# Twelve RMS norms of a two-block model: sums of squares in token columns, the root on 128x4 values, and the factor spread over the rows by a TensorE product

## The chip, the cores and the metric

The kernel runs on one core of a Trainium2 chip. The metric is the device time of one execution in microseconds, lower is better. A core has five engines that run side by side and meet at semaphores: TensorE (matrix products, PE in the profile, its weight loads PEld), VectorE (DVE), ScalarE (ACT), GpSimd (POOL) and SyncE (SP, which issues most transfers). SBUF is the working memory with 128 rows; TensorE writes only to PSUM, here eight banks of 128x512 fp32.

## The reference, cut to what matters

512 tokens of width 1024 go through two blocks, everything in fp32. Block one has two layers (latent attention, then attention with forget gates), each with a memory attention and an output projection whose result is normed and added to `x`. Block two has two layers, each a mixer and a gated feed-forward part, with a modulated norm ahead of each, and a norm at the end. Every norm is this one:

```python
def rms_norm(x, g):
    xf = x.astype(jnp.float32)
    y = xf * lax.rsqrt(jnp.mean(xf * xf, axis=-1, keepdims=True) + EPS)
    return (y * g.astype(jnp.float32)).astype(x.dtype)

def modulate(x, g, shift, scale):
    return (rmsnorm(x, g) * (1.0 + scale) + shift).astype(x.dtype)
```

The norms that the change touches, in order: the 256 memory tokens; `x` ahead of layer one; the query latent (width 384) and the key latent (256); the output of layer one, then `x` ahead of layer two; the output of layer two, then `x` ahead of the even mixer; `x` ahead of the first feed-forward part, of the odd mixer, of the second feed-forward part; the end. Twelve in all.

## The kernel before

The activations lie transposed: features on the 128 rows, tokens along the 512 columns, `x` as eight tiles of 128x512. Projections are fp32 products split in three (high times high, high times low, low times high). Weights arrive in a ring of three chunks; for each chunk ScalarE writes the high half `wh` (L1164), GpSimd the low half `wl` (L2024, 128x2048 for most), and TensorE multiplies (`three`, L505; `out_second`, L950). Two chunks of halves are in hand (SPLIT). Activations are split the same way: ScalarE writes the high half, VectorE the low half (`low`, L1596 or L1598). Each engine's program is written out in order by hand. TensorE takes its PSUM banks in rotation, six of them; bank seven, `ssq_bank`, is kept for the sums of squares and some attention outputs.

A norm goes like this. ScalarE squares a tile (`square`, L1189) into one of two buffers `sq`. TensorE multiplies it by a 128x128 matrix of ones (`ssq`, L532; for the memory L602 and L603), which sums over the features and at once puts the sum on all 128 rows: `ssq_bank` is 128x512. Where a norm is `summed`, VectorE has first added the squares of tiles 0 to 5 (`add_squares`), and TensorE has three products instead of eight (`ssq_summed`, L543). Then VectorE scales by 1/width and adds EPS (L1575), takes the reciprocal (L1578), ScalarE takes the root (`root`, L1202), all 128x512, in the tile `var`, which is also `rstd`. VectorE then multiplies tile by tile: `normed` (L1586), `normed_split` (L1619, with the high half on ScalarE and the low half on VectorE behind each tile), and in `out_first` L1736 for the output of a layer, followed by the addition to `x` (L1739), whose squares feed the next norm.

While this chain runs, TensorE has no projection to do. `warm(count)` (L448) gives it products of the identity with constants, each 512 columns, in fp32, which the profile shows as two passes: seven behind the last sum of an output norm, of the norm behind it and of the norms behind `out_second`, five between the sums of the two latent norms.

The lines around: in `out_first` ScalarE's order is square, copy, weight split (`split_weights`), root; VectorE's order there is the sums of pairs, L1575, L1578, L1736 and L1739 in turn. At the start TensorE does the sums of the memory, then those of `x`, then the memory projections (chunk `mem0`, which wait for nothing from the norm of `x`). In the latent part it does the three sums of the query latent, `warm(5)`, the two sums of the key latent, the rotation of the rotary key (L645), and the gate projections.

## Time and profile before

| | us |
|---|---|
| three runs | 2172.75, 2181.15, 2181.36 (median 2181.15) |
| the profiled execution | 2180.79 |
| its span | 2179.0 |
| TensorE busy | 2062.0 (95%) |
| TensorE loading weights | 1572.6 (72%) |
| VectorE busy | 1053.4 (48%) |
| ScalarE busy | 780.9 (36%) |
| GpSimd busy | 782.9 (36%) |

A line such as L505 is that of a helper, and many places of the program share it. The busy share of TensorE holds the filler products (94.2 us in 212 passes). The granted clock of TensorE is 0.976 in the mean. What a norm costs is not seen in these totals; it is read from the timeline, between the last sum and the first normed tile.

### The profile page before, as it was taken

Reading aid. Unit: us, or ns where it says so; the run is one execution under the profiler, and the core shown is the slowest. Engines: PE = TensorE matmul, PEld = TensorE weight load, DVE = VectorE, ACT = ScalarE, POOL = GpSimd, SP = SyncE. Lnnn points to the kernel's source line nnn. Section 1 sums busy time; section 2 is a strip of 40 time slices with the busy share of each in tenths; the row PEclk is TensorE's granted clock in tenths of the full one; section 3 lists DMA queues with packets and bytes.
Section 4 is the critical chain, followed back from the end, with each engine's and each line's share of the span. In section 5 each row is a group of like instructions: output and inputs, shape, how many; then the busy total and the mean of one; then the engine's idle time right before and its main releaser. Section 6 shows DMA issues by size and latency. Waiting matters only on the chain.

```text
span 2179.0 us, 22946 instructions
## 1 busy us (share of the span) xinstructions
PE 2062.0 (95%) x9468; PEld 1572.6 (72%) x9468; DVE 1053.4 (48%) x1507; ACT 780.9 (36%) x1186; POOL 782.9 (36%) x333
## 2 busy tenths in 40 slices
PE   7998999889999999997999998999999999999998
PEld 5765667588856679884778877886975577788886
DVE  6356575654466666914275546635601343211233
ACT  3332564423355332135342312324355433322231
POOL 3313363134354344221234334433423233434432
PEclk9999999999989999998999999999999999999999
DMA  5226202155510244110125344423311022233321
GB/s 177 90 89 161 78 1 68 60 175 173 174 59 21 97 135 136 59 59 20 58 77 160 111 134 137 149 90 97 97 59 39 20 97 78 78 97 98 108 62 62
DMA packets 202728, 203.54 MB, mean 93 GB/s; under 512 B 11871, under 2 KB 199523, under 8 KB 202624
## 3 DMA queue, kind: packets, MB, share of 16 engines
q1 hardware_dynamic: 200953, 200.90, 28.9%
q0 software_dynamic: 656, 1.01, 0.3%
q8 instruction: 75, 1.23, 0.3%
q10 hardware_dynamic: 1015, 0.16, 0.0%
q14 instruction: 29, 0.24, 0.0%
HBM read 199.10 MB, written 2.10 MB: 92 GB/s over the span
## 4 chain that ended last, share of the span: by engine, by line
PE 69%; DVE 14%; ACT 7%; POOL 6%; DMA 2%; issue 2%; SPq 0%; DVEq 0%; ACTq 0%; POOLq 0%
PE bank L505 40%; PE bank L950 14%; POOL wl L2024 6%; ACT wh L1164 3%; PE bank L687 2%; DVE var L1578 2%; DVE acc L1546 2%; PE bank L711 1%; PE bank L807 1%; PE bank L736 1%; DVE conv L1917 1%; DVE conv L1919 1%; PE bank L1009 1%; DVE conv L1915 1%; PE bank L1030 1%
## 5 line engine op out<-in xcount | busy, mean ns | idle before, releaser
L2024 POOL TENSOR_TENSOR wl<-ring,wh 128x2048 fp32r<-128x2048 f32 (+3 forms) x150 | 643.0, 4288 | 1099.3 <-ACT wh L1164 1099.3
L1164 ACT ACTIVATE wh<-ring 128x2048 fp32r<-128x2048 f32 (+3 forms) x150 | 265.1, 1768 | 286.1 <-PE bank L950 95.3
L1546 DVE SCALAR_TENSOR_TENSOR acc<-ring,cs,acc 128x256 f32<-128x256 f32 x336 | 287.5, 856 | 12.0
L505 PE MATMUL bank<-xfh,wh 128*128 128x512 f32 x704 | 278.2, 395 | 15.6 <-POOL wl L2024 12.7
L505 PE MATMUL bank<-xfh,wl 128*128 128x512 f32 x704 | 275.0, 391 | 0.0
L505 PE MATMUL bank<-xfl,wh 128*128 128x512 f32 x704 | 274.9, 391 | 0.0
L505 PEld LDWEIGHTS bank<-xfh,wh 128*128 128x128 f32 x704 | 132.6, 188 | 51.1 <-POOL wl L2024 17.4
L505 PEld LDWEIGHTS bank<-xfh,wl 128*128 128x128 f32 x704 | 132.6, 188 | 28.2
L1894 DVE SCALAR_TENSOR_TENSOR x<-bank,mod,x 128x512 f32<-128x512 f32 x48 | 34.7, 750 | 243.0 <-PE bank L950 243.0
L505 PEld LDWEIGHTS bank<-xfl,wh 128*128 128x128 f32 x704 | 132.8, 189 | 26.6
L950 PE MATMUL bank<-hsph,wh 128*128 128x512 f32 x352 | 138.8, 394 | 4.7 <-POOL wl L2024 4.7
L950 PE MATMUL bank<-hsph,wl 128*128 128x512 f32 x352 | 138.0, 392 | 0.0
L950 PE MATMUL bank<-hspl,wh 128*128 128x512 f32 x352 | 137.9, 392 | 0.0
L2043 POOL TENSOR_SCALAR probs<-probs,rinv 128x256 f32<-128x256 f32 (+2 forms) x96 | 95.4, 1007 | 70.1 <-DVE rinv L1713 70.1
L1915 DVE TENSOR_SCALAR conv<-a_raw,vecs 128x512 f32<-128x512 f32 x44 | 23.9, 544 | 192.4 <-ACT a_raw L1170 192.4
L1170 ACT ACTIVATE a_raw<-bank 128x512 f32<-128x512 f32 x44 | 26.5, 602 | 194.0 <-PE bank L505 192.2
L448 PE MATMUL bank<-consts 128*128 128x512 f32 x212 | 94.2, 593 | 0.0
L1544 DVE TENSOR_SCALAR acc<-ring,cs 128x256 f32<-128x256 f32 x48 | 24.3, 507 | 141.7 <-PE bank L495 131.7
L1280 ACT ACTIVATE probs<-bank,nmx 128x256 f32<-128x256 f32 (+3 forms) x128 | 64.5, 512 | 59.4 <-DVE nmx L1710 59.3
L1189 ACT ACTIVATE sq<-x 128x512 f32<-128x512 f32 x56 | 35.1, 630 | 129.2 <-DVE x L1894 116.1
L950 PEld LDWEIGHTS bank<-hsph,wh 128*128 128x128 f32 x352 | 66.8, 190 | 19.0 <-issue 4.8
L505 PE MATMUL bank<-xbh,wh 128*128 128x512 f32 x184 | 73.6, 400 | 3.6 <-DVE xbl L1596 3.6
(386 smaller groups left out, 4277.4 us busy)
## 6 DMA issues: line engine op xcount, KB each, us to landing
ring<-in_ada_w SPq DMA_DIRECT2D x48, 1024.0 KB, 5.3
ring<-in_ffn_w_in SPq DMA_DIRECT2D x44, 1024.0 KB, 5.2
ring<-in_w_in_b SPq DMA_DIRECT2D x14, 1024.0 KB, 5.3
ring<-in_even_w_in SPq DMA_DIRECT2D x14, 1024.0 KB, 5.2
ring<-in_ffn_w_out SPq DMA_DIRECT2D x16, 768.0 KB, 4.9
ring<-in_odd_w_in SPq DMA_DIRECT2D x12, 1024.0 KB, 5.3
ring<-in_ffn_w_out SPq DMA_DIRECT2D x16, 640.0 KB, 4.4
ring<-in_w_out SPq DMA_DIRECT2D x8, 1024.0 KB, 5.1
```

Source lines behind the costliest of these rows:

```text
L448: eng.matmul(b[:, :], ident, consts[:, 0:S], start=True, stop=True)
L505: mm = eng.matmul(o, l_, r_, start=(first and i == 0), stop=(last and i == 2))
L687: eng.matmul(b[:, at_col:at_col + n], qf[0:kd, h, i * P:n], kf[0:kd, h, 0:n], start=first, stop=False, skip_group_check=True)
L950: mm = eng.matmul(b[:, :], ws[a_][:, k, t * P:(t + 1) * P], xs[b_][:, k0 + k, :], start=(first and j == 0), stop=(end and j == 2))
L1164: eng.activation(wh[:, m % SPLIT, 0:w], ring[:, n % RING, 0:w], ACT.Copy).then_inc(wh_ready, 1)
L1189: eng.activation(sq[:, i % 2, :], src, ACT.Square).then_inc(sq_ready, 1)
L1280: ins = eng.activation(probs[:, par, po:po + n], b[:, c:c + n], ACT.Exp, bias=nmx[:, par, i:i + 1], scale=scale, accum_out=rsum[:, par, i: ...
L1546: ins = eng.scalar_tensor_tensor(out=s, in0=w[:, k, :], scalar=cs[:, k:k + 1], in1=s, op0=ALU.mult, op1=ALU.add)
L1578: eng.reciprocal(var[:, 0:n], var[:, 0:n]).then_inc(var_ready, 1)
L1915: chain.link(eng.tensor_scalar(u, r[:, 0:S], vec(name, t), vec("ffn_conv_b_2", FT * l + t), ALU.mult, ALU.add))
L2024: eng.tensor_tensor(wl[:, m % SPLIT, 0:w], ring[:, n % RING, 0:w], wh[:, m % SPLIT, 0:w].bitcast(F32), ALU.subtract).then_inc(wl_ready, 1)
L2043: eng.tensor_scalar(w, w, rinv[:, par, i:i + 1], None, ALU.mult).then_inc(probs_ready, 1)
```

## The change

- `token_sums` takes the place of the product with 128x128 ones. The square is now the stationary operand, 128 tokens at a time, and one column of ones the moving one: four products of one column for each tile. `ssq_bank` then holds 128x4 values (128x2 for the memory): the sum of token 128j+p on row p, column j.
- Scaling, reciprocal and root work on `rcol`, 128x4.
- VectorE writes `var`, 128x512: the identity times the column j of `rcol`, four diagonals side by side (`diag_ready`).
- TensorE multiplies ones by these diagonals (`spread`) into a rotating bank: the factor of each token on all rows. A `spread` stands in TensorE's program behind the sums of each norm: for the memory ahead of the sums of `x`, for `x` ahead of the memory projections, and for the two latent norms both behind the second latent's sums.
- `normed_split` and `out_first` read the factor from that bank, `normed` copies it to `var` first. The last tile frees the bank, so it counts on `emptied["dve"]` in place of `scaled` or `post_scaled`; waits and counts on the other engines follow.
- The filler: 7 and 7 in `out_first` become 1, spread, 2, and 1, spread, 2 (`OUT_FILL`), with one product of 256 columns behind each of the first seven sums of `x`; 7 behind `out_second` become 1, spread, 2.

```diff
@@ TensorE
-            def warm(count, aside=False):
+            def warm(count, aside=False, n=S):
@@
-                    eng.matmul(b[:, :], ident, consts[:, 0:S], start=True, stop=True)
+                    eng.matmul(b[:, 0:n], ident, consts[:, 0:n], start=True, stop=True)
@@
+            def token_sums(src, first, last, fold=1):
+                blocks = NB // fold
+                for j in range(NB):
+                    mm = eng.matmul(ssq_bank[:, j % blocks:j % blocks + 1], src[:, j * P:(j + 1) * P], ones[:, 0:1],
+                                    start=(first and j == 0), stop=(last and j >= NB - blocks),
+                                    skip_group_check=True)
+                mm.then_inc(sq_used, 1)
@@ ssq
-                eng.matmul(ssq_bank[:, :], ones, sq[:, i % 2, :], start=(t == 0), stop=(t == total - 1)
-                           ).then_inc(sq_used, 1)
+                token_sums(sq[:, i % 2, :], t == 0, t == total - 1)
                 counts["sq"] += 1
+            def spread(n=S):
+                k = counts["spread"]
+                b = bank(("rs", k), "dve")
+                pe.wait_ge(diag_ready, k + 1)
+                done(eng.matmul(b[:, 0:n], ones, var[:, 0:n], start=True, stop=True))
+                counts["spread"] += 1
@@ the start
             counts["hn"] += 1
+            spread(M)
             for k in range(KT):
                 ssq(k, KT)
+            spread()
@@ the latent norms
             warm(5)
             for t in range(2):
                 ssq(t, 2)
+            spread()
+            spread()
@@ out_first
                 ssq_summed()
-                warm(7)
+                warm(OUT_FILL[0])
+                spread()
+                warm(OUT_FILL[1])
                 for t in range(KT):
                     ssq(t, KT)
-                warm(7)
+                    if t < KT - 1:
+                        warm(1, n=M)
+                warm(OUT_FILL[2])
+                spread()
+                warm(OUT_FILL[3])
@@ out_second
                 if last:
                     ssq_summed()
-                    warm(7)
+                    warm(1)
+                    spread()
+                    warm(2)
@@ ScalarE, root
-                eng.activation(rstd[:, 0:n], var[:, 0:n], ACT.Sqrt).then_inc(rstd_ready, 1)
+                eng.activation(rcol[:, 0:n // P], rcol[:, 0:n // P], ACT.Sqrt).then_inc(rstd_ready, 1)
@@ VectorE, inverse
-                eng.tensor_scalar(var[:, 0:n], ssq_bank[:, 0:n], 1.0 / width, EPS, ALU.mult, ALU.add
+                cols = slice(0, n // P)
+                eng.tensor_scalar(rcol[:, cols], ssq_bank[:, cols], 1.0 / width, EPS, ALU.mult, ALU.add
                                   ).then_inc(ssq_taken, 1)
                 dve.wait_ge(ssq_taken, k + 1)
-                eng.reciprocal(var[:, 0:n], var[:, 0:n]).then_inc(var_ready, 1)
+                eng.reciprocal(rcol[:, cols], rcol[:, cols]).then_inc(var_ready, 1)
                 used["norm"] += 1
+                dve.wait_ge(rstd_ready, k + 1)
+                shape = [P, n // P, P]
+                eng.tensor_tensor(var[:, 0:n].rearrange("p (b q) -> p b q", q=P), ident.unsqueeze(1).to_broadcast(shape),
+                                  rcol[:, cols].unsqueeze(2).to_broadcast(shape), ALU.mult).then_inc(diag_ready, 1)
+                return take(dve, ("rs", k), "dve")
@@ normed
-                inverse(count, width, n, squares)
-                dve.wait_ge(rstd_ready, used["norm"])
+                b = inverse(count, width, n, squares)
+                eng.tensor_copy(var[:, 0:n], b[:, 0:n]).then_inc(emptied["dve"], 1)
+                wait_emptied(dve, ("rs", used["norm"] - 1))
@@ normed_split
-                    eng.scalar_tensor_tensor(out=tmp[:, t % 2, :], in0=x[:, t, :], scalar=g, in1=rstd[:, :],
-                                             op0=ALU.mult, op1=ALU.mult).then_inc(scaled, 1)
+                    eng.scalar_tensor_tensor(out=tmp[:, t % 2, :], in0=x[:, t, :], scalar=g, in1=rs[:, :],
+                                             op0=ALU.mult, op1=ALU.mult
+                                             ).then_inc(scaled if t < KT - 1 else emptied["dve"], 1)
@@ out_first
-                        eng.tensor_tensor(o1[:, t, :], o1[:, t, :], rstd[:, :], ALU.mult).then_inc(post_scaled, 1)
+                        eng.tensor_tensor(o1[:, t, :], o1[:, t, :], rs[:, :], ALU.mult
+                                          ).then_inc(post_scaled if t < KT - 1 else emptied["dve"], 1)
```

## Rows read from the trace of the kernel before

**Rows 1.** The chain that ended last, by engine, from the page.
```profile
PE 69%; DVE 14%; ACT 7%; POOL 6%; DMA 2%; issue 2%; SPq 0%; DVEq 0%; ACTq 0%; POOLq 0%
```

**Rows 2.** Groups by line and shape; busy us, mean ns, idle before.
```profile
L1578 DVE RECIPROCAL var<-var 128x512 f32<-128x512 f32 x11 | 36.9, 3353 | 0.4
```

**Rows 3.** Timeline, norm ahead of the first feed-forward part; start us, length us, what.
```profile
1089.44 0.30 PEld L532 LDWEIGHTS bank<-sq,consts 128*128 128x128 f32 x2 [0.61 <-ACT sq L1189]
...
1090.60 0.69 DVE L1575 TENSOR_SCALAR var<-bank 128x512 f32<-128x512 f32 x1 [1.88 <-PE bank L532]
...
1091.20 1.28 ACT L1202 ACT_TABLE_LOAD   x1
...
1091.26 4.51 POOL L2024 TENSOR_TENSOR wl<-ring,wh 128x2048 fp32r<-128x2048 f32 x1 [6.28 <-ACT wh L1164]
1091.33 3.35 DVE L1578 RECIPROCAL var<-var 128x512 f32<-128x512 f32 x1
...
1095.38 1.61 DVE L1619 SCALAR_TENSOR_TENSOR tmp_f<-x,gmod,var 128x512 f32<-128x512 f32 x2 [0.70 <-ACT var L1202]
```

**Rows 4.** Timeline, operations of 128x4 values at 776 us.
```profile
775.85 0.20 ACT L1360 ACTIVATE lbt<-lbt 128x4 f32<-128x4 f32 x1
...
776.09 0.18 DVE L1787 RECIPROCAL lbt<-lbt 128x4 f32<-128x4 f32 x1 [0.69 <-ACT lbt L1360]
```

**Rows 5.** Timeline at 49 and at 1145 us: GpSimd and VectorE at once.
```profile
48.97 4.51 POOL L2024 TENSOR_TENSOR wl<-ring,wh 128x2048 fp32r<-128x2048 f32 x1 [14.92 <-ACT wh L1164]
...
49.45 4.59 DVE L1596 TENSOR_TENSOR xal<-tmp_a,xah 128x512 fp32r<-128x512 f32 x1 [0.65 <-ACT xah L1176]
...
1145.29 5.03 POOL L2024 TENSOR_TENSOR wl<-ring,wh 128x2048 fp32r<-128x2048 f32 x1 [1.44 <-ACT wh L1164]
...
1145.99 1.29 DVE L1937 TENSOR_TENSOR prod<-bank,gel 128x512 f32<-128x512 f32 x2
```

**Rows 6.** Timeline of the output norm of layer one and the norm behind it.
```profile
390.34 4.51 POOL L2024 TENSOR_TENSOR wl<-ring,wh 128x2048 fp32r<-128x2048 f32 x1 [9.33 <-ACT wh L1164]
...
395.08 1.29 DVE L1736 TENSOR_TENSOR o<-o,var 128x512 f32<-128x512 f32 x2 [0.70 <-ACT var L1202]
...
397.69 0.30 PEld L532 LDWEIGHTS bank<-sq,consts 128*128 128x128 f32 x2 [2.25 <-ACT sq L1189]
...
398.90 0.30 PEld L532 LDWEIGHTS bank<-sq,consts 128*128 128x128 f32 x2 [0.91 <-ACT sq L1189]
...
406.94 0.69 DVE L1575 TENSOR_SCALAR var<-bank 128x512 f32<-128x512 f32 x1 [2.13 <-PE bank L532]
```

**Rows 7.** Timeline, four products with one moving column, eight weight loads.
```profile
194.06 1.09 PEld L495 LDWEIGHTS bank<-consts,acc 128*128 128x128 f32 x8
```

**Rows 8.** Timeline, a product with 256 moving columns, its two weight loads.
```profile
21.22 0.41 PEld L602 LDWEIGHTS bank<-sq,consts 128*128 128x128 f32 x2
```

**Rows 9.** Timeline of the two latent norms: last filler pass, first tiles.
```profile
131.05 0.19 PEld L448 LDWEIGHTS bank<-consts 128*128 128x128 f32 x1 [0.24 <-issue]
...
132.59 2.08 DVE L1586 SCALAR_TENSOR_TENSOR cq<-cq,vecs,var 128x512 f32<-128x512 f32 x3 [0.70 <-ACT var L1202]
...
141.16 1.41 DVE L1586 SCALAR_TENSOR_TENSOR ckv<-ckv,vecs,var 128x512 f32<-128x512 f32 x2 [0.70 <-ACT var L1202]
```

**Rows 10.** Timeline, the first memory projection.
```profile
37.55 0.19 PEld L505 LDWEIGHTS bank<-memh,wh 128*128 128x128 f32 x1 [2.46 <-issue]
```

**Rows 11.** Stretches: length; busy PE, PEld, DVE, ACT, POOL; PEclk, DMA share, GB/s.
```profile
788.50:792.70 4.20, 0.23 (x3) 0.14 (x2) 3.54 (x1) 1.15 (x3) 4.20 (x1) 0.75 0.75 238
790.60:797.40 6.80, 4.64 (x11) 3.67 (x12) 6.66 (x5) 3.19 (x2) 5.44 (x2) 0.50 0.59 193
397.70:406.00 8.30, 7.83 (x15) 2.38 (x16) 7.11 (x12) 4.41 (x7) 0.00 (x0) 1.00 0.20 69
```

**Rows 12.** Groups by line and shape: a factor from a bank, and from SBUF.
```profile
L1894 DVE SCALAR_TENSOR_TENSOR x<-bank,mod,x 128x512 f32<-128x512 f32 x48 | 34.7, 750 | 243.0 <-PE bank L950 243.0
...
L1619 DVE SCALAR_TENSOR_TENSOR tmp_f<-x,gmod,var 128x512 f32<-128x512 f32 x16 | 12.2, 775 | 1.8 <-ACT var L1202 1.4
```

49 lines of the change are left out of this document (27 added, 22 removed).

## The prediction

> **What bounds the kernel now.** I read the page first. The chain that ended last is TensorE work for 69% [rows 1], so at most places a change on VectorE or ScalarE costs nothing. The norms are the exception: between the last square and the first normed tile no projection can run. TensorE looks busy there, but only with `warm` filler. So I read each of the twelve norms in the timeline and asked what is late there. The largest item is the reciprocal, 3.353 us for 128x512, 11 times [rows 2]. In the norm ahead of the first feed-forward layer [rows 3] the last sum starts at 1089.44, the scaling (L1575) at 1090.60, the reciprocal at 1091.33, and the first normed tile at 1095.38: 4.78 us from the start of the scaling to the first tile. Two more things stand in these rows. ScalarE loads the table of the root at 1091.20 for 1.28 us, ready at 1092.48, which the reciprocal hides. GpSimd makes the low half of a weight chunk from 1091.26 to 1095.77.
>
> **Part 1, the chain without waits.** Scaling, reciprocal and root shrink to 128x4. The nearest rows are a 128x4 reciprocal, 0.18, and a 128x4 activation, 0.20 [rows 4]; for the scaling, which reads PSUM, I take 0.20 (bounds 0.16 to 0.69, the row before). Added are a 128x512 product onto the diagonals, 0.69 like every fp32 product here, and a TensorE product over 512 columns plus its wait. The old last sum had the same shape and took 1.16 from its first load to VectorE's start (1089.44 to 1090.60 [rows 3]). With 0.04 for each hand-over: 0.20+0.18+0.20+0.69+1.16+0.17 = 2.6 us instead of 4.78, 2.2 saved. `normed` copies the result out of PSUM first, 0.73 more, which leaves 1.4.
>
> **Part 2, the waiting product, the step that decides.** The diagonal product reads two tensors from SBUF, `ident` and `rcol`. Such an operation stands still here while GpSimd makes a low half: GpSimd works 48.97 to 53.48, and a 0.69 us subtraction issued at 49.45 takes 4.59, ending 0.55 after GpSimd. The product L1937, with one operand in PSUM, is not touched at 1145.99 in the middle of a GpSimd subtraction [rows 5]. The old chain was of the second kind (PSUM input, then a reciprocal, which ran at 3.35 under GpSimd [rows 3]). The new one can't start its product before the root, 1092.48+0.20, and GpSimd took hold at 1091.26. So it ends at 1095.77+0.55 = 1096.32, `ones` is loaded at 1096.37, and the first tile starts at 1097.53, not 1095.38. The old first tile was itself held a little (two tiles took 1.61), the new one isn't: the net is +1.95. The same picture holds before the odd mixer and the second feed-forward layer: three times. The Trainium skill, "SBUF — State Buffer", section "SBUF: two separate sides", says that a VectorE operation with two SBUF inputs and a GpSimd operation that reads SBUF exclude each other for the whole instruction. By that rule the broadcast operands, which no row here has in such a product, make no difference.
>
> After the output projections of block one GpSimd sits the same way, 390.34 to 394.85, and the first product of the old chain is at 395.08 [rows 6]. New: 394.85+0.55+0.05+1.16 = 396.61, +1.5. Behind it eight squares go to TensorE. They came every 1.21 us (397.69, 398.90), the last one 7.93 after the first, and the next scaling stood at 406.94. A sum is now four one-column products, eight loads. The loads of such products [rows 7] take 1.09 for eight with the last one's 0.19, so 0.90 to 1.0 a sum; its result is later by 0.13. The old sum took 0.86, so the sums by themselves cost nothing. But behind each stands a 256-column `warm`, two passes 0.22 apart [rows 8], 0.43. TensorE's period becomes 1.33, over VectorE's 1.21: 7 x 1.33 = 9.3 instead of 7.9. The second scaling is at 397.69+1.5+9.3+1.3 = 409.8, +2.9. That second norm has no GpSimd work near it and its table is loaded, so it earns 2.2. Net +0.7, twice.
>
> **Part 3, the order on TensorE.** In the latent norms `spread` stands behind the filler and the second sum. The filler's last pass begins at 131.05 [rows 9] and ends at 131.48; two sums, 133.3; product and hand-over, 134.5; copy, 135.2. The first tile was at 132.59: +2.6. The second of them then earns 1.4, and its first tile, 141.16, comes 1.2 late; a weight split waits behind it on ScalarE. At the start of the kernel the memory projection ran from 37.55 [rows 10] beside the norm of x. It now stands behind that norm's `spread`. I put the last squares 3 us later (the sums of x wait for the memory's `spread`, itself behind GpSimd), the projection at 43.2, and the next low half, which waits for ScalarE to empty it, 2.9 us later. Bounds for the start are 0 (the order hidden in the filler) and 6 (the whole shift passed on); I take 2.9 because ScalarE's queue, not TensorE's, fed the next chunk. The final norm earns 2.2-0.13-0.73 = 1.3.
>
> **Part 4, filler and clock.** `warm(7)` becomes one or two products around the spread. After the last sum and one filler TensorE has no work from about 1091.2 until 1096.4, and from 390.8 until 395.4. Gaps of that size cost clock in this trace: 4.2 us without work from 788.5, a mean grant of 0.75 inside, and then 6.8 us at 0.50 [rows 11], the lower level, 1.2 GHz. I counted seven gaps of 4.3 us or more behind the start of the kernel, and all seven show it. The sums of the output norm, about 70% dense from 397.7, hold 1.00. The new gaps are 4.6 (two), about 5.6 (three) and 6 (the latent norms). At the lower level the spread's two passes take 0.9 longer, right on the path: +0.9 for the latent norms, and three times +0.95 for the norms ahead of wide projections, which VectorE paces afterwards, so only 0 to 0.5 more there. After the output projections `warm(2)` takes 3.4 instead of 1.7 and holds up the first sums: +1.9 each.
>
> Reading the spread factor from PSUM I cost at nothing: 750 ns for the 128x512 scalar-tensor-tensor from a bank, 775 in the mean from SBUF [rows 12]. The Trainium skill, "VectorE: DVE Perf Modes", in the section on the TRN2 errata, gives a fixed part of 120 cycles for a PSUM source and 58 for SBUF; by that 64 tiles would cost some 4 us more (an estimate). The rows don't show it.
>
> **The sum.** Start 2.9, latent norms 1.2+0.9 = 2.1, output norms 2 x (0.7+1.9) = 5.2, three modulated norms 3 x (1.95+0.95) = 8.7, end -1.3: +17.6 us. I see no wait for a transfer that would absorb it: DMA is 2% of the chain, and the transfers follow VectorE's steps, which shift too. The profiled execution took 2180.79 (span 2179.0), 0.36 below the median of three. 2181.15+17.6 = 2198.8.
>
> **Rivals.**
> A. As above: 2199, 50%.
> B. The product is held, but the clock stays at 1.00. For it: the fillers were thinned, not dropped. Against: seven gaps of seven. 2.9+1.2+1.4+5.9-1.3 = +10.1: 2191, 20%.
> C, not slower: VectorE gets its access before GpSimd, or a broadcast operand doesn't count. The product would run as soon as the root is there, 1092.72; first tile 1094.6, -0.95 with the old hold, three times. After the output projections -1.4 before the sums, 0 after them, -2.2 behind the second norm, twice. 2.9+1.2-4.4-2.9-1.3 = -4.5: 2177, 15%. It decides if the product starts within a microsecond of the root. Against it: every two-SBUF product issued inside a low half in this trace was held.
> D, the change does what its chain promises everywhere: 12 x 2.2 less four copies of 0.73 = -23: 2158, 7%. It needs C and also that the order at the start and in the latent norms is hidden.
> E. More loss: the clock stays low through the sums and the first projection chunk, the start gives 6, or PSUM reads cost more: about +30, 2211, 8%.
>
> **Range and chances.** A and B hold 70%; to leave out no more than 2 in 10, C must be in: 2174 to 2212. A's own range is 2193 to 2206. A measurement tells about 0.5%, 11 us. Faster by more: D and a little of C, 10%. Within: most of C, half of B, the low edge of A, 30%. Slower: 60%.
>
> **What would show it.** The diagonal product 4 us long, or ending 0.5 us behind GpSimd, in five norms, and 0.69 in the others; first tiles near 1097.5 in place of 1095.4; sums 0.9 long, 1.33 apart in the output norms; granted clock 0.50 for 3 to 7 us behind each. If the product is 0.69 everywhere, the prediction is wrong at part 2; if the clock stays 1.00, at part 4.

## The result, and the profile after

| | before | after |
|---|---|---|
| median of the runs, us | 2179.18 (4 runs) | 2226.66 (4 runs) |
| range | 2172.75 to 2181.36 | 2223.54 to 2227.21 |
| ratio | | 1.022, 95% interval 1.0195 to 1.0245 |
| span of the profiled execution | 2179.0 | 2224.4 |
| TensorE's mean granted clock | 0.976 | 0.949 |

Slower, as forecast, but by 47 us and not by 17.6. 2226.66 lies outside the range of 2174 to 2212. First the page: its busy times, and the rows of the 40 slices for TensorE and its clock.

```profile
PE 2090.6 (94%) x9754; PEld 1623.9 (73%) x9754; DVE 1028.6 (46%) x1523; ACT 775.5 (35%) x1186; POOL 783.6 (35%) x333
...
PE   6989999989999999996999998998999999999998
...
PEclk7989999799999989998999999999999889999999
```

VectorE lost 25 us of work (1053.4 to 1028.6), which is what the change was made of. TensorE gained 29 (2062.0 to 2090.6) and stayed the engine that bounds. The mean clock gives the size of the matter: each us at the lower level (1.2 GHz, granted 0.50) takes half a us from the mean, so 2179.0 us at 0.976 hold 105 us of it, and 2224.4 us at 0.949 hold 227 us. The time at the lower level has doubled.

Next the timeline of the norm ahead of the first feed-forward layer in after, the one that [rows 3] show of before; here and below the columns are start, length, engine, line, operation, output and input, with the idle time before it and what ended that in brackets.

```profile
1120.88 0.16 DVE L1611 TENSOR_SCALAR rcol<-bank 128x4 f32<-128x4 f32 x1 [1.82 <-PE bank L531]
1121.08 0.18 DVE L1614 RECIPROCAL rcol<-rcol 128x4 f32<-128x4 f32 x1
1121.55 1.28 ACT L1234 ACT_TABLE_LOAD   x1
1121.61 4.50 POOL L2066 TENSOR_TENSOR wl<-ring,wh 128x2048 fp32r<-128x2048 f32 x1 [6.26 <-ACT wh L1192]
1122.84 0.20 ACT L1234 ACTIVATE rcol<-rcol 128x4 f32<-128x4 f32 x1
1123.08 3.57 DVE L1618 TENSOR_TENSOR var<-consts,rcol 128x512 f32<-128x512 f32 x1 [1.82 <-ACT rcol L1234]
1126.13 0.37 SPq L1162 DMA_DIRECT2D ring<-in_ffn_w_in  x1
1126.70 2.07 PE L551 MATMUL bank<-var,consts 128*128 128x512 f32 x2 [4.53 <-DVE var L1618]
1128.57 3.37 PE L450 MATMUL bank<-consts 128*128 128x512 f32 x4
1128.82 1.41 DVE L1657 SCALAR_TENSOR_TENSOR tmp_f<-x,gmod,bank 128x512 f32<-128x512 f32 x2 [2.17 <-PE bank L551]
```

This is the held product. It starts at 1123.08, inside GpSimd's low half (1121.61 to 1126.11), and ends at 1126.65, 0.54 behind it. Its work is 0.69, it took 3.57. From scaling to first tile there are 7.94 us, in [rows 3] 4.78: +3.2, of which 0.9 is the spread at the lower clock.

Now the token sums, which the prediction had called free. The first view is of TensorE's weight loads, at the start of the kernel and in the norm behind the output of layer one:

```profile
30.36 13.98 PEld L531 LDWEIGHTS bank<-consts,sq 128*128 128x128 f32 x64
...
422.29 1.08 PEld L531 LDWEIGHTS bank<-consts,sq 128*128 128x128 f32 x8
423.28 0.30 PEld L450 LDWEIGHTS bank<-consts 128*128 128x128 f32 x2
...
427.42 2.04 PEld L531 LDWEIGHTS bank<-consts,sq 128*128 128x128 f32 x8
429.34 0.55 PEld L450 LDWEIGHTS bank<-consts 128*128 128x128 f32 x2
429.98 2.04 PEld L531 LDWEIGHTS bank<-consts,sq 128*128 128x128 f32 x8
...
437.26 0.16 DVE L1611 TENSOR_SCALAR rcol<-bank 128x4 f32<-128x4 f32 x1 [9.96 <-PE bank L531]
```

The second view is of the same stretches and, in its last row, of the same sums in the norm behind the output of layer two: window and length; busy PE, PEld, DVE, ACT, POOL; granted clock, DMA share, GB/s.

```profile
29.70:44.00 14.30, 14.20 (x65) 14.05 (x65) 7.94 (x15) 6.03 (x14) 4.34 (x1) 0.50 0.48 148
421.60:425.00 3.40, 3.40 (x27) 3.27 (x27) 3.40 (x7) 1.39 (x3) 0.00 (x0) 1.00 0.01 2
425.00:437.30 12.30, 12.30 (x51) 11.49 (x50) 2.34 (x5) 2.39 (x4) 0.00 (x0) 0.50 0.00 0
776.60:786.80 10.20, 10.06 (x72) 8.91 (x71) 8.63 (x17) 5.04 (x8) 0.00 (x0) 1.00 0.01 2
```

At full clock a sum and its 256-column filler have a period of 1.32 (422.29 to 423.61), as forecast. At 425.0 the clock falls to 0.50 with TensorE busy 100% of the time, and the period becomes 2.56 (427.42 to 429.98), twice VectorE's 1.2 per tile. It had been at 0.50 from 411.3 to 421.6 too, behind the wait for the held product, and was back at 1.00 for the 3.4 us of the second row. One layer on the same sums keep 1.00 for 10.2 us, and the clock falls at 786.8, ahead of the last of the eight. At the start 64 loads take 13.98 us, one each 0.218, with TensorE busy 14.20 of 14.30 and the clock at 0.50 throughout; there it was low already when the sums began (from 25.6, in a gap of TensorE), and didn't come back while they ran. The engine looks full and runs at half its clock. That is the term that was missing.

To see where the time comes from I subtracted, for each of the 7200 passes of the split projections, its start in before from its start in the other kernel. The lateness (us) at some landmarks, given by their time in before. The columns x_a, x_b, x_even, ffn0 and ffn1 are the first passes on the normed `x` of layer one, layer two, the even mixer and the two feed-forward parts; 183.3 is a later chunk on x_a; x_odd lies 25 us behind the first pass on that of the odd mixer; 342.4 and 694.0 are the first passes of the two output projections. Kernels below the first row are those of the experiments:

| at | x_a 79.5 | first gate chunk 138.3 | 183.3 | 342.4 | x_b 414.0 | 694.0 | x_even 765.9 | ffn0 1098.0 | x_odd 1520.6 | ffn1 1791.3 |
|---|---|---|---|---|---|---|---|---|---|---|
| after | 8.3 | 22.6 | 17.2 | 20.1 | 29.2 | 24.6 | 29.6 | 33.2 | 36.4 | 46.0 |
| early_old | 0.0 | 0.0 | 0.1 | 1.0 | 6.0 | -4.0 | 2.7 | 6.3 | 10.0 | 19.4 |
| early_new | 7.8 | 22.1 | 16.5 | 19.5 | 22.1 | 19.3 | 22.1 | 19.5 | 19.5 | 19.5 |
| sums_128 | 6.4 | 17.5 | 11.3 | 14.7 | 17.6 | 6.8 | 9.2 | 10.0 | 12.9 | 22.5 |
| act_diag | 9.8 | 24.6 | 18.9 | 22.4 | 31.2 | 26.0 | 34.7 | 35.8 | 35.9 | 38.3 |
| root_first | 8.7 | 23.0 | 17.5 | 18.2 | 29.7 | 27.4 | 37.7 | 38.0 | 37.8 | 38.1 |
| order_1 | 8.1 | 8.9 | 20.7 | 23.2 | 28.2 | 25.5 | 34.6 | 35.9 | 37.8 | 45.4 |
| order_128 | 2.1 | -0.4 | 11.2 | 8.3 | 9.7 | 8.0 | 9.5 | 11.3 | 11.5 | 17.7 |
| combo | 0.7 | 0.7 | 0.6 | 0.8 | -0.5 | -10.0 | -11.3 | -13.0 | -14.3 | -11.1 |
| combo_table | 2.2 | 2.2 | 2.2 | 2.4 | 0.4 | -8.4 | -10.4 | -12.6 | -14.5 | -9.7 |
| combo_root | -0.3 | 1.3 | 1.9 | 2.1 | 5.1 | -5.0 | -3.6 | -1.0 | 0.8 | 5.9 |

Each row is one execution, so not every step is the edit's. The one of act_diag is the slowest of its four and 5 us above their median, that of combo is of the faster of its two groups of runs. The attention of layer two (414 to 694) is the same code in all of them. In before's profile the clock is at 0.50 from 609.7 to 626.8 with TensorE busy 17.10 of 17.10. In combo's it is 1.00 there:

```profile
600.00:650.00 50.00, 47.93 (x264) 28.27 (x264) 36.88 (x107) 32.24 (x113) 30.06 (x30) 1.00 0.20 64
```

That alone is about 9 us, and early_old, sums_128 and the three combos have it at that place. In the table sums_128 gains 6.2 us on after between 414.0 and 694.0 in this way, where their code is the same. So steps are read at the norms, where the rows of the timeline explain them, and sizes are taken from medians.

### The profile page after: what moved, and what is told of

Read it like the earlier page. It is cut to its first block, busy times and chain, and to the rows that moved or that the text cites. A ratio compares the mean times of both kernels' runs of the same rounds, so it can differ in the third digit from the quotient of the medians.

```text
span 2224.4 us, 23539 instructions
## 1 busy us (share of the span) xinstructions
PE 2090.6 (94%) x9754; PEld 1623.9 (73%) x9754; DVE 1028.6 (46%) x1523; ACT 775.5 (35%) x1186; POOL 783.6 (35%) x333
## 3 DMA queue, kind: packets, MB, share of 16 engines
q1 hardware_dynamic: 200953, 200.90, 28.2%
q8 instruction: 77, 1.26, 0.2%
## 4 chain that ended last, share of the span: by engine, by line
PE 72%; DVE 11%; ACT 7%; POOL 6%; DMA 2%; issue 2%; SPq 0%; DVEq 0%; ACTq 0%; POOLq 0%
PE bank L507 40%; PE bank L976 13%; POOL wl L2066 5%; ACT wh L1192 3%; PE bank L707 2%; PE bank L450 2%; PE bank L531 2%; DVE acc L1581 2%; PE bank L731 1%; DVE conv L1959 1%; PE bank L833 1%; DVE conv L1961 1%; PE bank L756 1%; PE bank L551 1%; DVE var L1618 1%
## 5 line engine op out<-in xcount | busy, mean ns | idle before, releaser
L1581 DVE SCALAR_TENSOR_TENSOR acc<-ring,cs,acc 128x256 f32<-128x256 f32 x336 | 282.8, 842 | 12.0
L1936 DVE SCALAR_TENSOR_TENSOR x<-bank,mod,x 128x512 f32<-128x512 f32 x48 | 34.7, 751 | 244.2 <-PE bank L976 244.2
L450 PE MATMUL bank<-consts 128*128 128x512 f32 (+1 forms) x176 | 96.7, 683 | 0.0
L976 PEld LDWEIGHTS bank<-hsph,wh 128*128 128x128 f32 x352 | 66.8, 190 | 19.3 <-issue 4.8
L976 PEld LDWEIGHTS bank<-hsph,wl 128*128 128x128 f32 x352 | 66.7, 190 | 14.0
```

Source lines behind the costliest of these rows:

```text
L450: eng.matmul(b[:, 0:n], ident, consts[:, 0:n], start=True, stop=True)
L976: mm = eng.matmul(b[:, :], ws[a_][:, k, t * P:(t + 1) * P], xs[b_][:, k0 + k, :], start=(first and j == 0), stop=(end and j == 2))
L1581: ins = eng.scalar_tensor_tensor(out=s, in0=w[:, k, :], scalar=cs[:, k:k + 1], in1=s, op0=ALU.mult, op1=ALU.add)
L1936: eng.scalar_tensor_tensor(out=x[:, t, :], in0=b[:, :], scalar=mod[:, col:col + 1], in1=x[:, t, :], op0=ALU.mult, op1=ALU.add).then_inc(em ...
```

## The experiments

The theory now had two parts. The held product costs, as predicted. And sums of one moving column let the clock fall although TensorE is never idle. The rivals: it is the thinned filler that lets the clock fall; or it is the order of TensorE's program at the start.

**early_old**: the first four norms as in before, the other eight as in after. The edit gives every norm both forms and picks by its number:

```diff
+NEW = (4, 5, 6, 7, 8, 9, 10, 11)
-                token_sums(sq[:, i % 2, :], t == 0, t == total - 1)
+                if counts["hn"] - 1 in NEW:
+                    token_sums(sq[:, i % 2, :], t == 0, t == total - 1)
+                else:
+                    eng.matmul(ssq_bank[:, :], ones, sq[:, i % 2, :], start=(t == 0), stop=(t == total - 1)
+                               ).then_inc(sq_used, 1)
...
```

> The changed kernel with its first four norms (memory, x, the two latents) made as before, the other eight as changed. The trace of the changed kernel shows the projections 19.6 us late at 206 us, ahead of the first attention. If that shift is made by the first four norms and nothing later takes it back, this run is about 19 us faster than the changed kernel: near 2208. If my prediction's sizes for these norms were right (2.9+2.1 = 5 us) and the rest is chance of the clock, it is near 2222.

Measured: 2196.6 (2192.2 to 2199.4), ratio 1.0073 [1.005, 1.0096], 30 us below after, and 11 below the 2208 expected. Taking the first four norms back to the old form gives back more than half of the loss. In the table after is 17 to 20 us late between 183.3 and 342.4, where I had counted 5.0. What it has beyond these comes next, in stretches that are the same in both kernels: 4.1 at the first output norm (steps of 9.1 and 5.0), 5.4 in the attention of layer two.

**early_new**: the other half, `NEW = (0, 1, 2, 3)`.

> Only the first four norms (memory, x, the two latents) as in the changed kernel, the other eight as before. Theory (parts add as the two traces show them side by side, 19.6 us of lateness where the second layer begins, some of it absorbed in the attention behind): 2195 to 2201, and the sum with early_old's 15 leaves about 10 of the changed kernel's 47 us to a loss that needs both. Rival (the losses of the two halves add to the whole): 2209 to 2214.

Measured: 2202.8 (2201.5 to 2208.7), ratio 1.0124 [1.0093, 1.0154]: +24.0 over the median of before in that comparison. With early_old's +15.4 that makes 39.4 of the 47.5. It fits neither number exactly: between the theory's 2201 and the rival's 2209, nearer to the theory. The 8 us that only both together lose have one visible part. In early_old seven of the eight sums of the norm behind layer one's output ran at full clock, 1.33 apart, and the clock fell at 411.6:

```profile
402.60 0.97 PEld L539 LDWEIGHTS bank<-consts,sq 128*128 128x128 f32 x8 [0.98 <-ACT sq L1244]
...
410.44 1.08 PEld L539 LDWEIGHTS bank<-consts,sq 128*128 128x128 f32 x8
```

so that the output norm and the next cost 5.0 us there (1.0 to 6.0 in the table), in after 9.1 (20.1 to 29.2). The same instructions lost the clock 9 us into the sums here and 5 us into them in after. What decides that I can't say from these runs.

**sums_128**: the ones are the moving operand with 128 columns and not with one. The sums are the same, 128 times over, and the scaling reads each 128th column. Nothing else is changed.

```diff
-                    mm = eng.matmul(ssq_bank[:, j % blocks:j % blocks + 1], src[:, j * P:(j + 1) * P], ones[:, 0:1],
+                    mm = eng.matmul(ssq_bank[:, (j % blocks) * P:(j % blocks) * P + 128], src[:, j * P:(j + 1) * P], ones[:, 0:128],
...
-                eng.tensor_scalar(rcol[:, cols], ssq_bank[:, cols], 1.0 / width, EPS, ALU.mult, ALU.add
+                eng.tensor_scalar(rcol[:, cols], ssq_bank[:, 0:n:P], 1.0 / width, EPS, ALU.mult, ALU.add
```

> The changed kernel with one edit: each product of the sums has 128 columns of ones moving instead of one, so the weight loads are the same, 0.112 us apart at full clock, and 128 columns are worked on behind each. Theory A (the clock falls because the one-column sums work on hardly any columns, though the profile calls the engine busy): the sums of x at the start, 64 loads in 13.98 us at a grant of 0.50, take about 7.3; the sums of x behind the output norm of layer one stay at 1.00; 10 to 15 us faster than the changed kernel, 2212 to 2217. Theory B (only the gaps without work lower the clock): the same stretches at 0.50 as in the changed kernel, and 2223 to 2229.

Measured: 2202.2 (2200.8 to 2205.4), ratio 1.0102 [1.0083, 1.0122]. Giving TensorE 128 times the columns made the kernel 24.4 us faster, more than the theory's 10 to 15. The 64 loads at the start now take 10.21 us, not the 7.3 expected; the clock is low for the first part only (mean grant 0.79 from 28 to 44, in after 0.50 from 29.7 to 44), and the sums of the output norm run at full clock to the end:

```profile
30.87 10.21 PEld L531 LDWEIGHTS bank<-consts,sq 128*128 128x128 f32 x64
...
28.00:44.00 16.00, 10.96 (x66) 10.47 (x66) 9.80 (x21) 8.06 (x18) 6.54 (x2) 0.79 0.42 132
...
425.49 1.08 PEld L531 LDWEIGHTS bank<-consts,sq 128*128 128x128 f32 x8
426.80 0.16 DVE L1611 TENSOR_SCALAR rcol<-bank 128x4 f32<-128x4 f32 x1 [3.38 <-PE bank L531]
```

A sum of eight loads takes 1.08 us at full clock with one column (after, 422.29 above) and with 128: the loads set the pace, and the columns are free. So the difference of 24.4 us can only be the clock and what hangs on it. How much of it lies in the sums is less sure: by the table 5.4 us come before 342.4, 6.2 at the first output norm, 6.2 in the untouched attention of layer two and 5.7 behind it. Without the attention it is some 18 us, an estimate from two single executions.

The traces of all kernels settle the direction. At the two output norms, each with 64 one-column products and fillers between them, six kernels (after, early_old, act_diag, root_first, order_1, fillers) give twelve stretches of sums. The clock fell inside eleven of them, and in the twelfth, of root_first, 0.4 ahead of its first load; it was low for 2.3 to 19.7 us of each. The six kernels with 128 columns (sums_128, order_128, the four combos) give twelve as well, and it fell inside none; in three it was low already when the sums began, for 1.4 to 6.2 us of them, and came back. At the start of the kernel the clock stays at 0.50 through all 14.0 us of one-column sums in five kernels, and with 128 columns it is back after 4.5 to 5.4 us in three.

**fillers**: one-column sums, but with six fillers in front of the spreads of the memory, the two output norms and the norms behind `out_second`, and five in front of the key latent's. The other four spreads stay as in after.

```diff
-OUT_FILL = (1, 2, 1, 2)
+OUT_FILL = (6, 2, 1, 2)
...
+            warm(6)
             spread(M)
...
+            warm(5)
             spread()
...
-                    warm(1)
+                    warm(6)
                     spread()
```

> The changed kernel with more filler: six products in place of one ahead of the spreads that wait for the held product (output norms, and the norms behind out_second), six ahead of the memory's spread, five between the two latent spreads. The order and the sums are as changed. Theory A (one-column sums lower the clock by themselves): the gaps hold 1.00, the spreads there take 1.2 instead of 2.2 us, but the sums of x at the start and behind the output norm still fall to 0.50; 5 to 10 us faster than the changed kernel, 2217 to 2222. Theory B (the gaps alone): the sums stay at 1.00 too, about 20 us faster, 2207.

Measured: 2217.3 (2212.9 to 2227.7), ratio 1.0176 [1.0144, 1.0208]. The clock theory's 2217 to 2222, not the rival's 2207. The six fillers at the start close the gap ahead of the sums, and these rows are the plainest of all: the clock is at 1.00 when the 64 loads begin at 30.84, and falls at 34.4 with TensorE busy without a break. The third row is of the norm behind layer two's output, at 0.50 with TensorE busy all the time:

```profile
29.00:34.40 5.40, 5.40 (x38) 4.40 (x36) 3.52 (x5) 1.72 (x3) 4.79 (x2) 1.00 0.59 194
34.40:48.00 13.60, 11.78 (x50) 10.69 (x51) 8.47 (x22) 5.98 (x15) 0.00 (x0) 0.50 0.26 78
...
764.90:785.40 20.50, 20.50 (x67) 15.67 (x66) 7.79 (x17) 4.69 (x8) 0.00 (x0) 0.50 0.00 0
```

Filler that replaces idle time gave back 9.4 us, columns in the sums 24.4. One of the four runs, at 2227.7, is no faster than after, so the size of the 9.4 is rough; that the thinned filler is the smaller part holds.

**act_diag**: ScalarE writes the diagonals, four copies of the identity scaled by a column, so that VectorE has no product of two SBUF tensors there.

```diff
                 eng.activation(rcol[:, 0:n // P], rcol[:, 0:n // P], ACT.Sqrt).then_inc(rstd_ready, 1)
+                act.wait_ge(rstd_ready, k + 1)
+                for j in range(n // P):
+                    ins = eng.activation(var[:, j * P:(j + 1) * P], ident, ACT.Copy, scale=rcol[:, j:j + 1])
+                ins.then_inc(diag_ready, 1)
...
-                eng.tensor_tensor(var[:, 0:n].rearrange("p (b q) -> p b q", q=P), ident.unsqueeze(1).to_broadcast(shape),
-                                  rcol[:, cols].unsqueeze(2).to_broadcast(shape), ALU.mult).then_inc(diag_ready, 1)
```

> The changed kernel with one edit: the diagonals are written by ScalarE right behind the root, four copies of the identity's 128 columns, each scaled by a column of rcol, so nothing of the chain can be held by GpSimd. If the hold costs what the trace shows (products of 3.57 to 4.99 us in five norms): spread's loads start 2.3 to 3.7 us sooner in these five, the gap without TensorE work falls from 5.2 to 5.9 us to about 3, some of them keep the clock, and the other seven norms pay 0.6 us each for the four copies: near 2212. If the hold is covered by something else that is late: 2226 to 2230.

Measured: 2213.8 (2207.6 to 2218.7), ratio 1.0144 [1.0118, 1.017], 12.9 below after. The timeline of the norm ahead of the first feed-forward layer:

```profile
1126.49 4.50 POOL L2066 TENSOR_TENSOR wl<-ring,wh 128x2048 fp32r<-128x2048 f32 x1 [6.26 <-ACT wh L1192]
...
1127.96 1.28 ACT L1237 ACTIVATE var<-consts,rcol 128x128 f32<-128x128 f32 x4
...
1131.41 1.41 DVE L1657 SCALAR_TENSOR_TENSOR tmp_f<-x,gmod,bank 128x512 f32<-128x512 f32 x2 [5.26 <-PE bank L551]
```

ScalarE wrote all four in 1.28 us in the middle of a GpSimd low half and wasn't held. In the table the three steps of after at ffn0, x_odd and ffn1 (3.6, 3.2, 9.6) are 1.1, 0.1 and 2.4. At the output norms nothing came back: their steps are 8.8 and 8.7 against 9.1 and 5.0, though scaling to first tile is 2.3 shorter in both. In the second of them the clock falls at 781.4 and not at 786.8.

**root_first**: the same hold taken off the product by time. ScalarE takes the root ahead of the weight chunk's high half, so GpSimd's low half comes after the product.

```diff
-                split_weights(tile_chunk[index[(stage, KT - 1)]] + 3)
                 root()
+                split_weights(tile_chunk[index[(stage, KT - 1)]] + 3)
...
-                split_weights(tile_chunk[index[stage + (KT - 1,)]] + 3)
                 root()
+                split_weights(tile_chunk[index[stage + (KT - 1,)]] + 3)
```

> As the changed kernel (2226.7), but ScalarE takes the root ahead of the weight chunk's high half in the two output norms and behind the three second projections, so that GpSimd's low half starts after the diagonal product. Theory (the product is held by GpSimd's low half and by nothing else): the product takes 0.69 in these five norms; first tiles 2.9 earlier three times, 1.5 twice: 2213 to 2217. Rival (the low half comes 2 us later and now holds VectorE's subtractions behind the first tiles, so that it is only moved): the product takes 0.69, but the time stays at 2221 to 2228.

Measured: 2215.7 (2204.9 to 2219.6), ratio 1.0161 [1.0133, 1.0189], 11.0 below after.

```profile
1128.92 0.69 DVE L1618 TENSOR_TENSOR var<-consts,rcol 128x512 f32<-128x512 f32 x1 [0.27 <-ACT rcol L1234]
...
1130.77 4.51 POOL L2066 TENSOR_TENSOR wl<-ring,wh 128x2048 fp32r<-128x2048 f32 x1 [8.03 <-ACT wh L1192]
...
1131.78 1.41 DVE L1657 SCALAR_TENSOR_TENSOR tmp_f<-x,gmod,bank 128x512 f32<-128x512 f32 x2 [2.17 <-PE bank L551]
1133.32 2.51 DVE L1640 SCALAR_TENSOR_TENSOR xfl<-tmp_f,mod,xfh 128x512 fp32r<-128x512 f32 x1
```

The product takes 0.69, and the steps at the three norms are gone (0.3, -0.2, 0.3), while those of the output norms grew to 11.5 and 10.3. The last line shows the rival at work too: the first subtraction of the low part, two SBUF inputs and more, is now the one that is held, 2.51 in place of 0.75. The same is true in all five norms: the first operation of two SBUF inputs behind the first tile takes 3.23 and 2.84 (the additions to `x` behind the output projections), 2.51, 3.40 and 2.50, for 0.68 to 0.75 of work. So root_first moved the hold off the first tile and didn't remove it. Both medians, 12.9 and 11.0, lie beside the 8.7 + 2 x 1.5 worked out. That the hold lies on the path is shown; its price isn't separated from the clock's by these two runs.

**order_128** and **order_1**: TensorE's order as in before at the two early places, on top of sums_128 and on top of after. The edit also drops the three fillers (`fill=3`) that stood ahead of the first gate chunk in before and in after.

```diff
             for k in range(KT):
                 ssq(k, KT)
-            spread()
...
                 wide([("km", l, c) for c in range(2)], "act", ws, (mh, ml), KT, "mem", n=M)
                 chunk_done(m)
+                if not l:
+                    spread()
...
             for t in range(2):
                 ssq(t, 2)
             spread()
+            m, ws = chunk("in_a.gate")
+            wide([("in_a.gate", t) for t in range(2)], "act", ws, xa, KT, "x_a")
+            chunk_done(m)
+            ada_sums(1)
             spread()
...
-            project("in_a.gate", 4, "act", "x_a", xa, lag=1, fill=3)
+            for t in range(2, 8, 2):
...
```

> As sums_128 (2202.2), but TensorE's order is put back to what it was in the kernel before at two places: the spread of x's norm stands behind the first memory chunk, not ahead of it, and the spread of the key latent behind the first gate chunk. Theory (in the early part it is the order on TensorE that costs, not the clock of the sums): of the 14 us of lateness that sums_128 shows ahead of the output projections about 8 to 12 go: 2190 to 2194. Rival (the lateness comes from VectorE's and ScalarE's longer chain, the spreads stand wherever they stand): 2199 to 2203.

> As the changed kernel (2226.7), with one-column sums, but TensorE's old order at the two early places, as in order_128. Theory (order and clock are separate costs): 5 to 8 us less, as between sums_128 and order_128: 2218 to 2222. Rival (the order costs more where the clock is low, because the sums of x stand ahead of the memory projection for 14 us): 2209 to 2216.

Measured: order_128 2196.1 (2190.4 to 2202.3), ratio 1.0079 [1.005, 1.0107], 6.1 below sums_128. order_1 2219.6 (2209.6 to 2224.5), ratio 1.0189 [1.0153, 1.0226], 7.1 below after. By the medians the order costs 6 to 7 us at either clock. With four runs each that is not firm: order_1's range is 15 us wide, and its profiled execution is nearly as slow as after's (spans of 2222.6 and 2224.4; 45.4 and 46.0 late at ffn1). That order and clock are separate costs is likely and not shown. The 6.1 is less than the 8 to 12 that I expected of order_128, and its trace says why. Weight loads of the gate projection's first and second chunk, then ScalarE's high half of the second:

```profile
137.91 0.19 PEld L507 LDWEIGHTS bank<-xah,wh 128*128 128x128 f32 x1 [0.24 <-issue]
...
161.19 0.29 PEld L507 LDWEIGHTS bank<-xah,wh 128*128 128x128 f32 x1 [10.86 <-POOL wl L2075]
...
151.82 1.29 ACT L1213 ACTIVATE ckvsh<-ckv 128x512 fp32r<-128x512 f32 x2 [8.14 <-DVE ckv L1637]
...
154.54 1.89 ACT L1201 ACTIVATE wh<-ring 128x2048 fp32r<-128x2048 f32 x1
```

The first chunk is on time again (137.91, in before 138.26). The second waits 10.86 us for its low half, because its high half stands on ScalarE behind the high part of the key latent (144.66 in before, 154.54 here), and that waits for VectorE's spread factor, whose product I had put behind the first chunk. At 183.3 the table has 11.2, as in sums_128 (11.3), and 20.7 in order_1 against 17.2 in after. The lateness only changed its place in the order, from TensorE to ScalarE.

**combo**: the mends together where they should bring a gain: norms 5 to 12 the new way, 128 columns, diagonals by ScalarE, the first four as before. **combo_order**: all twelve norms the new way with all three mends.

> The first four norms (memory, x, the two latents) as before, the other eight the new way, with 128 moving columns in the token sums and the diagonals written by ScalarE (four 128x128 copies scaled by a column). Theory (the two costs are separate and add): early_old stood at 2196.6; without the three held products (2.9 each behind it) and without the loss of clock behind the one-column sums (4 to 6) this gives 2181 to 2185, no difference from before, granted clock near 0.975. Rival (what is freed is absorbed by the next thing that is late, such as the weights' low halves): 2188 to 2193.

> All twelve norms the new way, with all three mends: 128 moving columns, the diagonals by ScalarE, TensorE's old order at the two early places. If the three are separate: combo's time plus what the early part still costs, 4 to 8 us for the longer chains of the first four norms: 2185 to 2192. If the order gives nothing: 2195 to 2199.

Measured: combo 2177.4 (2166.2 to 2185.4, 12 runs), ratio 0.9981 [0.9963, 0.9999]. combo_order 2178.4 (2169.3 to 2188.6, 10 runs), ratio 1.0004 [0.9983, 1.0024]. The first is 4 us below what the separate costs gave, the second 7. Combo's runs form two groups, five from 2166.2 to 2168.8 and seven from 2177.1 to 2185.4, so its mean, 2174.7, says more than its median; the differences of 4 and 7 are no more than such a step can make, and the costs add as far as these runs can tell. The loss of 47 us is taken back in full by the three mends, with the change still in: 128 columns, no held product, and TensorE's order.

**combo_table** and **combo_root**: in combo, in the norm ahead of the first feed-forward layer, the chain from scaling to first tile is no shorter than in [rows 3], 4.97 to their 4.78, since the reciprocal of 3.35 had hidden ScalarE's weight chunk and table load, and these now stand bare. It is the longest of the five; the others have 3.89 twice (output norms), 4.58 and 3.16:

```profile
1077.61 0.16 DVE L1650 TENSOR_SCALAR rcol<-bank 128x4 f32<-128x4 f32 x1 [1.93 <-PE bank L539]
...
1076.26 1.89 ACT L1215 ACTIVATE wh<-ring 128x2048 fp32r<-128x2048 f32 x1
1078.17 1.28 ACT L1258 ACT_TABLE_LOAD   x1
1079.46 0.20 ACT L1258 ACTIVATE rcol<-rcol 128x4 f32<-128x4 f32 x1
...
1082.58 1.41 DVE L1693 SCALAR_TENSOR_TENSOR tmp_f<-x,gmod,bank 128x512 f32<-128x512 f32 x2 [4.59 <-PE bank L566]
```

combo_table adds to combo a root of one column two tiles before the last square, so that the table is there. combo_root also moves the root ahead of the chunk and gives the diagonals back to VectorE.

```diff
+                    if t == KT - 2:
+                        eng.activation(spare[:, 0:1], ident[:, 0:1], ACT.Sqrt)
                     square(x[:, t, :], t)
```

> As combo (2177.4), with a root of one column placed on ScalarE two tiles ahead of the last square in the output norms and the second projections, so that the table of the root is loaded there. In combo the table load of 1.28 stands between the weight chunk's high half and the root, and nothing on VectorE is long enough to hide it now. Theory: 1.2 to 1.3 saved in five norms, 2170 to 2173. Rival (the load is moved ahead of a square that is itself on the path, or TensorE's filler ends no earlier): 2176 to 2179.

> As combo_table, but the diagonals by VectorE again (one 128x512 product) and the root ahead of the weight chunk's high half as in root_first. Theory: neither the table, nor the high half, nor GpSimd stands in the chain any more; from the scaling to the first tile about 2.7 instead of 4.97 in combo, at five norms, of which the two output norms gain half: 2166 to 2170. Rival (GpSimd's low half starts 2 us later and holds VectorE's subtractions behind the first tiles): 2175 to 2181.

Measured: combo_table 2169.2 (2164.3 to 2175.5, 12 runs), ratio 0.9962 [0.9945, 0.9978], 8 us below combo by the medians, 5 by the means (2169.5 and 2174.7), and the clearest gain over before, 0.4%. From scaling to first tile it takes 3.16 (1079.53 to 1082.69), and 3.14 to 3.16 in all five norms, together 4.7 less than in combo. combo_root 2187.6 (2181.8 to 2193.6, 12 runs), ratio 1.0044 [1.0026, 1.0063]: slower, and beyond even the rival's 2181. Its chain is the shortest of all, 2.55 from scaling (1089.29) to first tile:

```profile
1091.84 1.41 DVE L1695 SCALAR_TENSOR_TENSOR tmp_f<-x,gmod,bank 128x512 f32<-128x512 f32 x2 [1.22 <-PE bank L567]
1093.38 3.46 DVE L1678 SCALAR_TENSOR_TENSOR xfl<-tmp_f,mod,xfh 128x512 fp32r<-128x512 f32 x1
...
1091.78 4.51 POOL L2106 TENSOR_TENSOR wl<-ring,wh 128x2048 fp32r<-128x2048 f32 x1 [8.13 <-ACT wh L1216]
```

and the gain is gone with the next instruction. GpSimd starts 0.06 before the first tile, and the subtraction behind it takes 3.46. In combo_table GpSimd works from 1080.15 to 1084.68, most of it while VectorE waits for the spread anyway, and the same subtraction takes 1.00. In all five norms of combo_root the first operation with two SBUF inputs behind the first tile takes 3.40 to 3.79 in place of 0.7, and in the table combo_root's steps there are 5.0, 3.4, 4.8, 3.7 and 0.3 above combo_table's, 17 of the 18 us between them. Here the chain up to the first tile is the wrong measure. What counts is the time at which the low parts are out.

## Why the prediction was right or wrong

**Right: part 2, the waiting product.** The diagonal product took 3.57 in four norms and 4.99 in the fifth, ending 0.5 behind GpSimd, and 0.69 elsewhere at 128x512. The five norms and the length were forecast. The broadcast operands made no difference. The Trainium skill, "SBUF — State Buffer", section "SBUF: two separate sides", gives just this exclusion, and the trace agrees (3.57 for a work of 0.69). Rival C falls with it, though the sign that I gave for it, a product that starts within a microsecond of the root, is met: it starts 0.04 behind the root (1123.04 to 1123.08 above), and the hold is in its length. At single norms the table has +3.6 and +3.2 with the clock's share, where 2.9 was forecast. The total fits as well, 11.7 worked out and 11.0 and 12.9 given back, but part of that is luck. By the table act_diag takes 12.8 us from the three modulated norms, 7.2 of them at ffn1, and loses 3.4 at the output norms, where 3.0 should have come back; and root_first only moved the hold.

**Right: the spread at the lower clock.** Ten of the twelve spreads in after took 2.1 to 2.2 from their load to VectorE's start (1126.70 to 1128.82 above), where the old sum took 1.16 [rows 3]. The 0.9 was forecast. The memory's, over 256 columns, took 1.26, and the query latent's ran at full clock, 1.17. The seven gaps of before that cost clock go down to 4.0 us (788.73 to 792.76), not 4.3; the seven new ones of after, 4.2 to 6.0 us, all did as well.

**Right: no cost in reading PSUM.** The modulated scalar-tensor-tensor takes 747 ns in the mean from a bank, against 775 in [rows 12]; that mean has the slightly held tiles in it, but the medians, 748 and 752, say the same. The Trainium skill, "VectorE: DVE Perf Modes", in its errata section, has a larger fixed part for a PSUM source. The rows of after don't show it:

```profile
L1657 DVE SCALAR_TENSOR_TENSOR tmp_f<-x,gmod,bank 128x512 f32<-128x512 f32 x16 | 11.8, 747 | 4.8 <-PE bank L551 4.3
```

**Wrong: "the sums by themselves cost nothing."** I priced a sum from [rows 7] and [rows 8], at full clock, and asked of the clock only how long TensorE's gaps were. The sentence that failed is the one in part 4 that "the sums of the output norm, about 70% dense from 397.7, hold 1.00". That row was of 512-column products in before (and it has TensorE busy for 7.83 of 8.30 us, 94%; my 70% was the 0.86 of a sum over its 1.21). I carried its clock over to products of one column, because both look busy in the profile. In after the sums are 100% dense by the profile, more than in before, and the clock falls in the midst of them. sums_128, with loads, waits and order unchanged, prices it at 24.4 us, some 18 of them without the untouched attention. Nothing in my sum stood for that; rival E had "the clock stays low through the sums", with about +30 and 8%, and its time of 2211 was still 16 short.

**Wrong: the start.** Counted at 2.9, with 6 as the bound, measured 8.3 at x_a. With the old order it is 8.1 at one column and 2.1 at 128 columns, with the new order and 128 columns 6.4. Either alone is enough to make most of the lateness at this place; only both mends remove it. My bound of 6 was that of the order alone.

**Wrong: the latent norms.** Counted at 2.1, measured about 9 (8.3 to 17.2). Two things were missed. The clock is at 0.50 from 134.9 to 141.7, from the query latent's sums on, so the five fillers between the latents took longer and the first spread came late: the first tile of the query latent at 147.39, 14.8 after [rows 9], of which 8.3 was there at the entry. And the prediction leaves out the first gate chunk. In before it is on TensorE from 138.26, beside the key latent's norm, whose first tile is at 141.16. Two spreads in front of it take that cover away: 22.6 late at this chunk.

```profile
146.66 0.69 DVE L1625 COPY var<-bank 128x512 f32<-128x512 f32 x1 [7.93 <-PE bank L551]
147.39 2.08 DVE L1628 SCALAR_TENSOR_TENSOR cq<-cq,vecs,var 128x512 f32<-128x512 f32 x3
...
152.63 0.50 PEld L551 LDWEIGHTS bank<-var,consts 128*128 128x128 f32 x2 [6.84 <-issue]
154.64 0.18 PEld L665 LDWEIGHTS bank<-kr,consts 32*32 32x32 f32 x2 [1.50 <-issue]
```

**Mis-sized: the output norms.** 5.2 for both pairs, measured 9.1 and 5.0, together 14.1 (the table, 342.4 to 414.0 and 694.0 to 765.9). The period of 1.33 was right as long as the clock was full; at the lower clock it is 2.56, and the second scaling came at 437.26. The second pair kept the clock through seven of its eight sums, and cost 5.0 where 2.6 was forecast.

**Mis-sized: the end.** From scaling to first normed tile 4.24 us (2206.90 to 2211.14) where it was 4.78, 0.5 earned and not 1.3, because that spread too ran at the lower clock (2.13).

**Open.** ffn1 stands 9.6 behind x_odd in after, and 9.4 in early_old, 9.6 in sums_128. The norm itself explains 3. Some 5 more are the clock in the odd mixer, at 0.50 for 3.4, 3.4 and 13.6 us (from 1728.9, 1739.1 and 1769.9), in before for 10.2 (from 1729.3) alone. The mixer's code is untouched. That it loses less in act_diag, root_first and combo_root is seen (2.4, 0.3, 5.1), but no run tells whether that is an effect of the norm ahead of it or chance, nor what the 8 us are that early_new and early_old leave over, nor why one-column sums lost the clock sooner in one norm than in another.

## What to carry over

- Price an operation on TensorE at both levels of its clock, and take the clock from rows of the same kind of operation. "Busy" in the profile doesn't say that the clock will hold: products of one column kept the engine 100% busy, and sooner or later in each of the twelve long stretches the clock was at 0.50; the same products with 128 columns took no longer at full clock (1.08 us for eight loads), lost it in none, and the kernel was 24 us faster.
- When a long operation on the path is cut, list what it was hiding (here a table load of 1.28, a weight chunk of 1.9, a low half of 4.5), and take these out as well or little is gained: at the five norms 3.16 to 4.97 in combo and 3.14 to 3.16 in combo_table, 4.78 before. And follow the chain beyond its first output, to the next operation that can be held.

## What the runs showed of the hardware that was not expected

- TensorE's granted clock fell from 1.00 to 0.50 at 425.0 with the profile showing it 100% busy with one-column products and short fillers, and it stayed at 0.50 through 14 us of such products at the start, 99% busy. In fillers it fell at 34.4, 3.6 us into such products, with no gap before it. With 128 moving columns the same loads held 1.00 in that output norm, and the clock fell inside none of the twelve stretches of output sums in six kernels.
- Eight loads with their fp32 products take 1.08 us at full clock with one moving column or with 128. At the lower level, with one column, they take 2.04.
- Four ScalarE copies of 128x128 scaled by a column take 1.28 us and are not held by GpSimd; one VectorE product of 128x512 onto the same tile takes 0.69 and is held for up to 4.99.
- In one execution an untouched attention stretch spends 17.1 us at 0.50 with TensorE fully busy, and in another none. A difference of 10 us between two single traces can be that.
